# Odd mixer: head norms under the input projection, two heads at a time, probabilities divided and turned by one product with a diagonal matrix

## The reference

```
h = rmsnorm(x, mix_norm[1]);  q, k, v, u = split(h @ odd_w_in, 4)        # 512 columns each
q, k = rmsnorm over each head's 64 channels (8 heads), with gains
scores = q k^T / 8 + rel_bias[h, clip(distance, -128, 128)]              # chunks of 64 tokens
a chunk sees itself and all chunks before it (8 to the left): everything to its left here
y_c = softmax(scores) @ v
y_d = per group of 128 channels: (trailing mean over 2/4/8/16 tokens - u) @ pool_w * pool_scale
x = x + concat(y_c, y_d) @ odd_w_out
```

## Time and profile before

| | us |
|---|---|
| median of 3 runs (lowest, highest) | 3274.4 (3270.32, 3275.35) |
| the profiled execution | 3276.05 |
| its span | 3274.3 |
| PE, DVE, ACT, POOL busy | 3100.9, 1470.4, 958.7, 195.8 |
| mean granted clock | 0.933 |

### The profile page before, as it was taken

One profiled execution on the slowest core, in us unless ns is written; L12 is line 12 of the kernel. 1 busy time (PEld: TensorE's weight loads), 2 busy tenths in 40 slices (PEclk: granted clock), 3 DMA queues, 4 the chain that ended last, 5 costly groups with the idle time before them and its releaser, 6 DMA issues. The chain is left out here.

```text
span 3274.3 us, 34803 instructions
## 1 busy us (share of the span) xinstructions
PE 3100.9 (95%) x12909; PEld 2418.5 (74%) x12924; DVE 1470.4 (45%) x1902; ACT 958.7 (29%) x1276; POOL 195.8 (6%) x211
## 2 busy tenths in 40 slices
PE   6999998789999999999999999999999999889997
PEld 5777876468888788887556888877776777568885
DVE  5574355564443444433223544327873334443323
ACT  4422232233332333221112333222223333233222
POOL 3000040010000000010200000000000000100000
PEclk9999997689999999999557999999998899989998
DMA  3334262123332233323001323334420013223321
GB/s 129 109 120 156 82 186 66 48 74 103 96 110 90 82 96 96 106 68 133 0 1 39 97 96 103 110 104 125 132 64 1 1 58 103 71 79 99 103 100 43
DMA packets 82850, 284.69 MB, mean 87 GB/s; under 512 B 14760, under 2 KB 15400, under 8 KB 82000
## 3 DMA queue, kind: packets, MB, share of 16 engines
q1 hardware_dynamic: 71392, 250.63, 24.0%
q0 software_dynamic: 6768, 26.70, 2.6%
q10 hardware_dynamic: 4608, 6.30, 0.7%
HBM read 262.35 MB, written 14.94 MB: 85 GB/s over the span
## 5 line engine op out<-in xcount | busy, mean ns | idle before, releaser
L177 DVE TENSOR_TENSOR wl<-raw,wh 128x1024 fp32r<-128x1024 f32 (+2 forms) x440 | 573.7, 1305 | 1047.8 <-ACT wh L171 1037.2
L200 PE MATMUL PS<-Hh,wl 128*128 128x512 f32 x2360 | 928.0, 393 | 40.9 <-DVE wl L177 18.0
L201 PE MATMUL PS<-Hh,wh 128*128 128x512 f32 x2360 | 921.3, 390 | 0.0
L202 PE MATMUL PS<-Hl,wh 128*128 128x512 f32 x2360 | 921.2, 390 | 0.0
L171 ACT ACTIVATE wh<-raw 128x1024 fp32r<-128x1024 f32 (+2 forms) x440 | 480.2, 1091 | 1147.6 <-PE PS L202 1030.8
L200 PEld LDWEIGHTS PS<-Hh,wl 128*128 128x128 f32 x2360 | 444.8, 188 | 149.4 <-issue 34.8
L202 PEld LDWEIGHTS PS<-Hl,wh 128*128 128x128 f32 x2360 | 444.7, 188 | 93.2
L201 PEld LDWEIGHTS PS<-Hh,wh 128*128 128x128 f32 x2360 | 445.0, 189 | 92.3 <-issue 1.0
L202 PE MATMUL PS<-ffn_gl,wh 128*128 128x512 f32 x880 | 351.0, 399 | 0.0
L200 PE MATMUL PS<-ffn_gh,wl 128*128 128x512 f32 x880 | 346.7, 394 | 2.6 <-DVE wl L177 2.6
L201 PE MATMUL PS<-ffn_gh,wh 128*128 128x512 f32 x880 | 347.1, 394 | 0.0
(11 more groups left out here) (401 smaller groups left out, 2884.3 us busy)
## 6 DMA issues: line engine op xcount, KB each, us to landing
raw<-in_gu SPq DMA_DIRECT2D x220, 512.0 KB, 3.5
raw<-in_dn SPq DMA_DIRECT2D x80, 704.0 KB, 4.0
raw<-in_hin SPq DMA_DIRECT2D x44, 512.0 KB, 3.8
raw<-in_oin SPq DMA_DIRECT2D x16, 512.0 KB, 3.6
raw<-in_hin_gate SPq DMA_DIRECT2D x16, 512.0 KB, 3.5
X<-QKV ACTq DMA_DIRECT2D x96, 64.0 KB, 2.9
kept_x<-X POOLq DMA_DIRECT2D x16, 256.0 KB, 3.6
raw<-in_eout SPq DMA_DIRECT2D x8, 512.0 KB, 3.6
```

The source lines that it names most:

```text
L177: self.nc.vector.tensor_sub(self.wl[j % SPLIT][:, 0:kw], self.raw[j][:, 0:kw], self.wh[j % SPLIT][:, 0:kw].bitcast(F32)).then_inc(self.lo_ ...
L200: self.nc.tensor.matmul(out, wl, xh[:, u.k0 + k, :], start=first, stop=False)
L201: self.nc.tensor.matmul(out, wh, xh[:, u.k0 + k, :], start=False, stop=False)
L202: done = self.nc.tensor.matmul(out, wh, xl[:, u.k0 + k, :], start=False, stop=last)
```

## The change

The columns of the input weights come in another order: u, q, k, and then v with tokens as the stationary side, so that v is made with tokens on partitions and needs no transposes (`token_unit`). Head norms move under the input projection: after each unit from the sixth on, PE sums the squares of one 128-channel block of q or k by one 512-column product with the block matrix `co.heads`, ACT takes the root, DVE inverts all 512 columns and multiplies. The trailing means on POOL move there too. The bias with its mask is a stored 128x512 tile a head (2 MB in all), of which the last (t+1) x 128 columns are used.

`chunk_attend` takes 16 steps of two heads: two score products into two banks, DVE's add of the bias with the running maximum in one instruction, exponentials in place in SBUF, and instead of scaling and transposing, a product of each block with a diagonal matrix of the inverse sums. Value products of the two heads alternate, into output partitions 0-63 and 64-127. The four pooling products and their splits stand in the last two iterations (`pooled_half` and what reads it, left out here; operations as before, with two tiles in place of four).

```diff
+        def token_unit(i, j):
...
+            pe.wait_ge(self.lo_ready, st.base + j + 1 + RAW * i)
+            for kk in range(2):
...
+                for t in range(TT):
+                    if k == 0:
+                        pe.wait_ge(bank_free, after + st.chunks * (i - lag) + t + 1)
+                    out, sel = self.PS[:, bank + t, :], tokens(t)
+                    self.nc.tensor.matmul(out, xh[:, k, sel], wl, start=k == 0, stop=False)
+                    self.nc.tensor.matmul(out, xh[:, k, sel], wh, start=False, stop=False)
+                    done = self.nc.tensor.matmul(out, xl[:, k, sel], wh, start=False, stop=k == DC - 1)
+            done.then_inc(self.unit_done, 1)
...
-def head_norms(co, QK, V, SEL, n, q_chunks, cols):
...
+def odd_input(co, st, QK, V, UU, windows, cols, loads):
...
+            windows.pool(pool, u_ready)
...
+            def total(n):
+                if n == 3:
...
+                if 5 <= n <= 12:
+                    k = n - 5
+                    pe.wait_ge(squared, k + 1)
+                    if k >= 2:
+                        pe.wait_ge(scaled, k - 1)
+                    nc.tensor.matmul(co.PS[:, 4 + k % 2, :], co.heads, SQ[:, k % 2, :], start=True,
+                                     stop=True).then_inc(summed, 1)
+            co.multiply(pe, st, bank_free, between=total)
...
+            def root(k):
+                act.wait_ge(scaled, k + 1)
+                nc.scalar.activation(R[:, k % 2, :], R[:, k % 2, :], ACT.Sqrt).then_inc(rooted, 1)
+            def read(i, c):
+                if i in (1, 2):
+                    k = RAW * (i - 1) + c
+                    act.wait_ge(taken, k + 1)
+                    if k >= 2:
+                        act.wait_ge(summed, k - 1)
+                    nc.scalar.activation(SQ[:, k % 2, :], QK[:, k, :], ACT.Square).then_inc(squared, 1)
+                    if k >= 1:
+                        root(k - 1)
+                if i == 3 and c == 0:
+                    root(7)
+                if i == 3 and c == 3:
+                    co.wait_units(act, st, i, c)
+                    act.wait_ge(copied, 1)
+                    for t in range(TT):
+                        nc.scalar.activation(V[:, t, :], co.PS[:, t, :], ACT.Identity,
+                                             scale=RSC[:, t:t + 1]).then_inc(stored, 1)
...
+            def scale(k):
+                dve.wait_ge(summed, k + 1)
+                if k >= 2:
+                    dve.wait_ge(normed, k - 1)
+                v.tensor_scalar(R[:, k % 2, :], co.PS[:, 4 + k % 2, :], ...).then_inc(scaled, 1)
+            def norm(k):
+                dve.wait_ge(rooted, k + 1)
+                v.reciprocal(R[:, k % 2, :], R[:, k % 2, :]).then_inc(inverted, 1)
+                dve.wait_ge(inverted, k + 1)
...
+                v.scalar_tensor_tensor(QK[:, k, :], QK[:, k, :], co.cols[:, g:g + 1], R[:, k % 2, :],
+                                       ALU.mult, ALU.mult).then_inc(normed, 1)
+            def read(i, c):
+                if i == 0:
+                    co.wait_units(dve, st, i, c)
+                    v.tensor_mul(UU[:, c, :], co.PS[:, c, :], co.RS[:]).then_inc(u_ready, 1)
+                    dve.wait_ge(u_ready, c + 1)
+                    dve.sem_inc(bank_free, 1)
+                if i == 1 and c == 0:
+                    dve.wait_ge(spread, 1)
+                    v.tensor_copy(RSC[:], co.PS[:, 6, 0:TT]).then_inc(copied, 1)
+                if i in (1, 2):
+                    k = RAW * (i - 1) + c
+                    co.wait_units(dve, st, i, c)
+                    v.tensor_mul(QK[:, k, :], co.PS[:, c, :], co.RS[:]).then_inc(taken, 1)
+                    dve.wait_ge(taken, k + 1)
+                    dve.sem_inc(bank_free, 1)
+                    if k >= 1:
+                        scale(k - 1)
+                    if k >= 2:
+                        norm(k - 2)
+                if i == 3 and c == 0:
+                    norm(6)
+                    scale(7)
+                if i == 3 and c == 1:
+                    norm(7)
...
+def chunk_attend(co, QK, V, BIAS, M, POOLED, PW, cols):
...
+            def scores(k):
+                c, t = steps[k]
+                w = width(k)
+                if k >= 2:
+                    pe.wait_ge(biased, 2 * (k - 2) + 2)
+                for s in range(2):
+                    r = HD * s
+                    nc.tensor.matmul(co.PS[:, 2 * (k % 2) + s, 0:w], QK[r:r + HD, c, t * P:(t + 1) * P],
+                                     QK[r:r + HD, 4 + c, 0:w], start=True, stop=True).then_inc(scored, 1)
+            def turn(k):
+                for s in range(2):
+                    pe.wait_ge(normed, 2 * k + s + 1)
+                    if k >= 1:
+                        pe.wait_ge(copied, 2 * (k - 1) + s + 1)
+                    for j in range(steps[k][1] + 1):
+                        m = nc.tensor.matmul(co.PS[:, 4 + s, j * P:(j + 1) * P], SC[:, k % 3, s, j * P:(j + 1) * P],
+                                             DG[:, k % 3, s, :], start=True, stop=True)
+                    m.then_inc(turned, 1)
+            def weigh(k):
+                c, t = steps[k]
+                pe.wait_ge(copied, 2 * k + 2)
+                if t == 0 and c >= 2:
+                    pe.wait_ge(out_lo, c - 1)
+                for j in range(t + 1):
+                    for s in range(2):
+                        h = 2 * c + s
+                        m = nc.tensor.matmul(co.PS[HD * s:HD * s + HD, 6 + c % 2, t * P:(t + 1) * P],
+                                             V[:, j, h * HD:(h + 1) * HD], PT[:, k % 2, s, j * P:(j + 1) * P],
+                                             start=j == 0, stop=j == t)
+                m.then_inc(weighted, 1)
...
+            for k in range(n + 3):
+                if k < n:
+                    scores(k)
+                if 2 <= k < n + 2:
+                    turn(k - 2)
+                if k >= n + 1:
+                    for g in (2 * (k - n - 1), 2 * (k - n - 1) + 1):
+                        pooled_half(g)
+                if k >= 3:
+                    weigh(k - 3)
...
+            for k in range(n + 3):
+                if k < n:
+                    w = width(k)
+                    act.wait_ge(negated, k + 1)
+                    for s in range(2):
+                        nc.scalar.activation(SC[:, k % 3, s, 0:w], SC[:, k % 3, s, 0:w], ACT.Exp,
+                                             bias=ST[:, k % 3, 1, s:s + 1], accum_out=ST[:, k % 3, 2, s:s + 1]).then_inc(powered, 1)
+                if 2 <= k < n + 2:
+                    w = width(k - 2)
+                    if k >= 4:
+                        act.wait_ge(weighted, k - 3)
+                    for s in range(2):
+                        act.wait_ge(turned, 2 * (k - 2) + s + 1)
+                        nc.scalar.activation(PT[:, k % 2, s, 0:w], co.PS[:, 4 + s, 0:w], ACT.Copy).then_inc(copied, 1)
...
+                if k >= 3 and steps[k - 3][1] == TT - 1:
+                    c = steps[k - 3][0]
+                    act.wait_ge(weighted, k - 2)
+                    nc.scalar.activation(M[0][:, c, :], co.PS[:, 6 + c % 2, :], ACT.Copy).then_inc(out_hi, 1)
...
+            for k in range(n + 3):
+                if k < n:
+                    c, t = steps[k]
+                    w = width(k)
+                    if k >= 3:
+                        dve.wait_ge(turned, 2 * (k - 3) + 2)
+                    for s in range(2):
+                        dve.wait_ge(scored, 2 * k + s + 1)
+                        v.tensor_tensor_reduce(SC[:, k % 3, s, 0:w], co.PS[:, 2 * (k % 2) + s, 0:w],
+                                               BIAS[:, 2 * c + s, S - w:S], op0=ALU.add, op1=ALU.max, scale=1.0,
+                                               scalar=NEG, accum_out=ST[:, k % 3, 0, s:s + 1]).then_inc(biased, 1)
+                    dve.wait_ge(biased, 2 * k + 2)
+                    v.tensor_scalar(ST[:, k % 3, 1, :], ST[:, k % 3, 0, :], -1.0, None, ALU.mult).then_inc(negated, 1)
+                if 1 <= k < n + 1:
+                    b = (k - 1) % 3
+                    dve.wait_ge(powered, 2 * k)
+                    v.reciprocal(ST[:, b, 3, :], ST[:, b, 2, :]).then_inc(inverted, 1)
+                    dve.wait_ge(inverted, k)
+                    for s in range(2):
+                        v.tensor_scalar(DG[:, b, s, :], co.ident, ST[:, b, 3, s:s + 1], None, ALU.mult).then_inc(normed, 1)
...
+                if k >= 4 and steps[k - 4][1] == TT - 1 or k == n + 2:
+                    c = steps[min(k - 4, n - 1)][0] if k < n + 2 else 3
+                    dve.wait_ge(out_hi, c + 1)
+                    v.tensor_sub(M[1][:, c, :], co.PS[:, 6 + c % 2, :], M[0][:, c, :].bitcast(F32)).then_inc(out_lo, 1)
...
+    st.tokens = {3: (lambda t: slice(t * P, (t + 1) * P), 0, 0)}
...
-        copy_stage(co, st_in, scaled_to(co, QU), scaled=True, loads=[
...
-        head_norms(co, QU[:, 0:8, :], QU[:, 8:12, :], SEL, 8, 4, cols)
...
```

(50 more changed lines are left out.)

207 lines of the change are left out of this document (98 added, 109 removed).

## The result

The changed kernel takes 3131.1 us (median of 4 runs, 3125.4 to 3133.4) against 3273.5 for the kernel before, timed beside it (4 runs, 3270.3 to 3275.4): ratio 0.9563, 95% interval 0.9547 to 0.9580, 142.4 us faster. The profiled execution took 3133.3 us, span 3131.5.

A forecast was written before the change was run, and what follows sets the result against it. PE's stream and its half clock were taken to bound attention, small-step chains the head norms. Gain 197.9 − A, 120 us at A = 78, took the profiled 3276.05 to 3156, median 3154 us; range 3139 to 3184.

The forecast's parts named there:

- The formula: Odd mixer: 214.6 us gone, 11.8 + 1 + 3.9 + A in their place, so gain 197.9 − A, 120 us.
- A: Attention with pooling, first score to first output product: 65 us at full clock, 100 at half, 78 forecast.
- Input stage: Input projection with the norms moved beside it: VectorE sets 6.85 us a unit; +11.8 us, plus 1 for GpSimd.
- the late split of unit 14: Input projection, before unit 14: split_hi stands behind root(7) in a chain, so the split comes 2.5 us late.
- VectorE and ScalarE beside PE: Attention with pooling: VectorE about 40 us, ScalarE 42, both under PE; reduces with add 17.
- Which clock: Attention's granted clock: 20 us at half, then 28% at half, making 78 us instead of 65.
- nearest relative of the new mix: Hybrid attention, taken as clock model for the new stage: 0.55 in its first 22 us, then 0.86.
- Rival 3: Attention at full clock all through: 65 us, gain 133, 3141 us; chance 0.12.
- The prediction's evidence against it: Old attention's transposes: 0.92 straight behind them, held against the skill's sentence that transpose mode never engages full clock.
- The price of half clock: Attention with pooling: 65 us at full clock, 100 at half; 20 us at half do 20/100 of the work.
- Size of A at full clock: Attention with pooling: PE work 53.1 us, 8.6 waiting for copies, 2.2 last rounding, 0.8 barrier: 65 us.
- The overlap of row groups: Two heads' scores on separate row halves: three passes' worth of four, 12.8 us at full clock, 25.6 at half.

The follow-up runs named there:

- b1_noflip: The kernel before without the bias product through the flip matrix, one-row mask product kept: 3226.2 us, ratio 0.9855, A 136.1 us, clock in attention 0.50.
- h1_oldattn: The changed kernel's new input stage with the attention and pooling of the kernel before: 3252.8 us, ratio 0.9940, A 178.3 us, clock 0.50.
- a1_warm: The changed kernel with four float32 products of 512 columns added right behind the last input product: 3132.5 us, ratio 0.9573, A 60.0 us.
- a1_transpose: The changed kernel with probabilities scaled by VectorE and transposed, in place of products by a diagonal matrix: 3139.9 us, ratio 0.9582, A 63.5 us.
- b1_dg: The kernel before with only its turn changed, from scaling and transposing to products by a diagonal matrix: 3223.4 us, ratio 0.9843, A 126.9 us.
- b1_neither: The kernel before without the mask product and without the flip (bias) product: 3212.5 us, ratio 0.9810, A 116.4 us, clock 0.50.
- b1_neither_dg: The kernel before without mask and flip products, and with the turn by diagonal-matrix products: 3199.1 us, ratio 0.9771, A 93.4 us.
- b1_nomask: The kernel before without the one-row mask product of each score, flip product kept: 3194.2 us, ratio 0.9756, A 96.4 us.
- a1_best: The changed kernel plus four products in the gap, values read by both engines, second head's copy on VectorE: 3133.1 us, ratio 0.9576, A 58.5 us.
- a1_trapart: The changed kernel with transposes for the turn and no overlap of score or value products: 3154.1 us, ratio 0.9622, A 75.9 us.
- a1_apart: The changed kernel with both heads' scores on the same rows and value products one head after the other: 3145.9 us, ratio 0.9612, A 70.4 us.

## Why the prediction was right in part and wrong in size

- **The formula held.** Gain 197.9 − A: with the measured A of 60.0 it gives 138; the profile shows 139 from the first input product to the first output product (input +12.3, gap and head norms −31.8, attention and pooling −119.1), and some 3.5 us ahead of the mixer, where nothing was changed and where the profiled kernels scatter by as much.
- **Input stage: right.** +12.3 us against 11.8 + 1; the reciprocal 3.34 against 3.35; the gap 3.77 against 3.9; the late split of unit 14 costs PE 1.8 us against 2.5. Splits that come late earlier on cost 0.5 and 0.9 us, where four times 0.4 had been taken.
- **VectorE and ScalarE beside PE: right.** Reduces with add 0.69 at 512 columns, 14.4 us in all and 2.7 more for their readouts against 17, diagonals 0.28 against 0.25 to 0.35, both under PE. PE's idle time in A is 9.1 us against 11.6. b1_noflip and h1_oldattn show the parts behaving as priced when the clock does not move.
- **Which clock: the step that failed.** The prediction took the hybrid attention as the "nearest relative of the new mix" and went on: "I take the same course: 20 us at half do 20/100 of the work", the rest at 28% half. That put 13 us on top of the 65 at full clock. What the new stage has is 6.8 us at half at its start and 1.00 from there on, and this cost 1.5 us. So 11 to 12 of the 18 us by which A was too long come from this step. The relative turns by transposes; the new stage turns by ordinary products, and in each of the kernels of this mixer that do so, the old attention too, the clock rises and then stays up, but for a short stretch near the end in some (a1_warm). With transposes in their place (a1_transpose) the mean is 0.74, about the 0.77 of the assumed course. Rival 3 (full clock all through, 3141) was the nearer one, and had 0.12. Its reason ("turns are twice as much streaming as transposes") fits b1_dg, where more streaming came with a higher clock; that the streaming is what raises it was not tested.
- **What was set aside on the way.** The Trainium skill ("TensorE: Matmul & The Clock Gate", Part 4, PE-mode transpose) says that full clock does not engage in transpose mode. Two pairs support it: b1_neither (0.50) and b1_neither_dg (0.99 after 30 us), and the kernel before (0.50) and b1_dg (1.00 after 27 us). It does not say what a mix does: b1_nomask is at 0.98 with its 80 transposes. The prediction's evidence against it, 0.92 straight behind 16 transposes, does not repeat. The same head norms stand in the five kernels made from the one before, and there the clock behind the transposes is 0.50, as here in b1_nomask:

```profile
1555.30:1559.30 4.00, 4.00 (x22) 4.00 (x20) 2.48 (x4) 1.81 (x4) 0.00 (x0) 0.50 0.02 4
```

- **The price of half clock: right, as far as shown.** "A = 65 us at full clock, 100 at half" makes a microsecond at half cost 0.35. Measured are 1.5 us for 6.8 (2.4 by this rate) where PE waits for other engines, 1.5 for 3.4 (1.2 by this rate) near the end, and up to 12 against 13 in a1_transpose.
- **Size of A at full clock: 6.5 us too long.** a1_best, at 1.00 throughout, and a1_warm without its low stretch have 58.5. a1_best has PE busy 48.0 us and idle 10.6, against 53.1 and 11.6 in the sum. The overlap of row groups was taken as three passes of four; it is two (1.13 us against 1.98 apart). One pass less in each of the 16 pairs is 4.3 us (an estimate, 320 columns on average at 0.83 ns a pass).

The chain of steps from 179.1 to 60.0 us in A: the turn by products −52 (b1_dg), flip and mask products gone from that −33 (b1_neither_dg), and the rest of the change −33, which is two heads at a time with pooling drawn in, the bias in VectorE's reduce, and the new front. In another order the shares differ, since the clock makes them depend on each other: the same removal of flip and mask is −63 at half clock without the turn. The last step isn't divided further: b1_neither_dg begins its attention at 0.50 and has 30 us of it, the changed kernel has 7, and no run tells how much of that the front does and how much the order of two heads.

What stays open: which property of the mix decides when the clock rises. The turn by products is sufficient in every kernel of this mixer that has it, and not necessary (b1_nomask, a1_trapart, a1_transpose rise too, later or in part), and the hybrid mixer's 0.87 shows that it does not make full clock by itself.

## What to carry to other kernels

Where PE is busy all the time and its granted clock still stands at half, try making its instructions fuller before making them fewer: one exchange of 80 transposes for products by a diagonal matrix, more work for PE, was worth 50 us, and taking full-height products away can cost time (b1_neither, without the flip products too, is 18 us slower than b1_nomask, and A is 20 us longer). Try it on the chip, stage by stage: where the clock is already at 0.84, the same exchange cost 23 us. And where PE waits for other engines, part of a longer PE stream goes into shorter waits: a1_apart has 14.5 us more PE work than the changed kernel, and A is 10.5 us longer. Before you call a change worthless by a total, compare the two runs at a point inside the stage.

## What the hardware showed that was not expected

- A stage with PE busy in 169.6 of 170.0 us is at 0.50 throughout. The same attention with the one-row products left out is at 0.98 from 9 us on (b1_nomask), and with another kind of turn at 1.00 from 27 us on (b1_dg).
- Products of 64 rows from disjoint row halves run at once, pass beside pass: four passes in 1.13 us, 1.98 when both use the same rows.
- An idle gap of 3.8 us was followed by 0.59 in the next 8 us; with four products in it the clock stayed at 1.00 there, and the stage was 1.5 us ahead.
